# Turning rows with DMA transposes in SBUF instead of TensorE, and one output product moved, in a hybrid attention/gMLP encoder block

## The reference

```
a = rmsnorm(x) @ w_in                  -> q (512), k (128), v (128), zu (512), zv (512)
attn = windowed attention, 8 query heads on 2 kv heads, +-128 tokens, ALiBi, sink logits
sgu  = gelu(zu) * (w_s @ layernorm(gelu(zv)) + b_s)        (within chunks of 128 tokens)
h = x + concat(rmsnorm(attn), rmsnorm(sgu)) @ w_out
gate, val = rmsnorm(h) @ w_up          (2816 columns each; gate: convolution over 3 tokens)
h = h + (gelu(conv(gate)) * val) @ w_down
h = h + (p @ w_ple_proj) * sigmoid(rmsnorm(h) @ w_ple_gate)
out = rmsnorm(h) * g_final
```

## Time and profile before

| | us |
|---|---|
| median of 3 runs (slowest core) | 1627.82 (1625.87 to 1628.7) |
| the profiled execution, its own time | 1642.0 |
| its span on the slowest core (core 7) | 1640.4 |
| its span on the fastest core (core 3) | 1617.9 |
| TensorE matmul busy, core 7 | 1556.9 (95%) |
| VectorE, ScalarE, GpSimd busy, core 7 | 929.4, 755.8, 433.3 |

### The profile page before, as it was taken

The page is one execution under the profiler, slowest core; times in us unless marked ns, Lnnn a source line. Parts: engine busy times, 40 slices in busy tenths (PEclk is TensorE's granted clock), DMA queues, the critical chain, the costliest instruction groups (busy, mean ns, idle before and its releaser), DMA issues.

```text
span 1640.4 us, 32602 instructions; the slowest of 8 cores (1617.9 to 1640.4 us)
## 1 busy us (share of the span) xinstructions
PE 1556.9 (95%) x11608; PEld 1038.4 (63%) x11608; DVE 929.4 (57%) x1765; ACT 755.8 (46%) x1351; POOL 433.3 (26%) x816
## 2 busy tenths in 40 slices
PE   1899998999998999999999999999999999999997
PEld 1455555555554775867768577685766857668573
DVE  1555556566565654745647466474654746556464
ACT  2554555565565443534435344353543535434242
POOL 2345556565553310111101111011111101110011
PEclk9887899999999999999999999999999999999998
DMA  9745446453328931120211102021120211201011
GB/s 175 157 103 119 105 128 128 130 122 89 89 65 166 202 89 39 43 65 17 82 34 48 56 26 81 19 64 46 37 81 15 67 39 43 81 9 48 14 43 52
DMA packets 32495, 123.78 MB, mean 75 GB/s; under 512 B 4144, under 2 KB 6352, under 8 KB 30288
## 3 DMA queue, kind: packets, MB, share of 16 engines
q1 hardware_dynamic: 24096, 85.22, 15.7%
q0 software_dynamic: 8240, 36.49, 14.3%
HBM read 124.62 MB, written 33.55 MB: 96 GB/s over the span
## 4 chain that ended last, share of the span: by engine, by line
PE 86%; DMA 6%; ACT 3%; issue 2%; DVE 2%; POOL 0%; DVEq 0%; POOLq 0%; ACTq 0%; SPq 0%
PE ps L244 86%; DMA big<-w_in_b 2%; ACT big L244 2%; DVE big L244 2%; DMA hmid<-big 2%; DMA big<-w_down 1%; ACT L244 1%; POOL big L244 0%; POOL big L144 0%; DVEq L169 0%; POOLq L161 0%; ACTq L169 0%; POOLq L169 0%; ACTq L161 0%; SPq L169 0%
## 5 line engine op out<-in xcount | busy, mean ns | idle before, releaser
L244 PE MATMUL ps<-big 128*128 128x256 bf16 (+5 forms) x11608 | 1556.9, 296 | 71.4 <-POOL big L244 31.8
L244 PEld LDWEIGHTS ps<-big 128*128 128x128 bf16 x11608 | 1038.4, 99 | 589.3 <-issue 157.4
L244 POOL TENSOR_SCALAR big<-big 128x1 f32<-128x1 f32 (+6 forms) x512 | 270.8, 534 | 1123.5 <-ACT big L244 1028.0
L244 ACT ACTIVATE big<-ps,big 128x256 f32<-128x256 f32 (+2 forms) x476 | 335.2, 707 | 330.9 <-PE ps L244 322.6
L244 DVE SCALAR_TENSOR_TENSOR big<-ps,big 128x256 f32<-128x256 f32 x704 | 338.7, 483 | 147.0 <-ACT big L244 108.0
L244 ACT ACTIVATE big<-big 128x256 bf16<-128x256 f32 (+3 forms) x553 | 317.8, 585 | 187.7 <-DVE big L244 174.6
L244 DVE TENSOR_TENSOR big<-ps,big 128x8 f32<-128x8 f32 (+3 forms) x176 | 146.9, 836 | 250.8 <-PE ps L244 243.6
L244 ACT ACTIVATE big<-ps 128x1024 bf16<-128x1024 bf16 (+2 forms) x96 | 78.0, 813 | 310.4 <-PE ps L244 308.5
L244 DVE SCALAR_TENSOR_TENSOR big<-big 128x1024 f32<-128x1024 f32 (+2 forms) x128 | 129.3, 1011 | 55.7 <-POOL big L244 46.9
L244 DVE TENSOR_TENSOR big<-big,ps 128x256 bf16<-128x256 bf16 x352 | 144.8, 411 | 5.6 <-ACT big L244 5.6
L244 POOL TENSOR_TENSOR big<-big 128x1 f32<-128x1 f32 (+1 forms) x224 | 126.5, 565 | 34.3 <-POOL big L244 1.7
(11 more groups left out here) (20 smaller groups left out, 32.3 us busy)
## 6 DMA issues: line engine op xcount, KB each, us to landing
big<-hmid SPq DMA_DIRECT2D x64, 512.0 KB, 6.2
big<-x SPq DMA_DIRECT2D x32, 512.0 KB, 3.7
hmid<-big SPq DMA_DIRECT2D x32, 512.0 KB, 2.9
out<-big SPq DMA_DIRECT2D x32, 512.0 KB, 3.1
big<-xT POOLq DMA_DIRECT2D x16, 512.0 KB, 6.7
big<-w_up POOLq DMA_DIRECT2D x8, 1024.0 KB, 12.8
big<-w_down POOLq DMA_DIRECT2D x2, 1792.0 KB, 22.5
big<-w_up POOLq DMA_DIRECT2D x4, 768.0 KB, 14.4
```

Of the source, the lines that this page charges most:

```text
L244: return S.op(eng, lambda e: getattr(e, fname)(*args, **kw), reads=r, writes=w, what=(fname, args, kw))
```

## The change

All three turnings are done by one DMA transpose each, from SBUF to SBUF, on SP's queue (`dmat`, which calls `dma_start_transpose`). So that one DMA can read a whole merged row, the attention half and the gMLP half now lie side by side in one buffer of 1024 (`mg_r`, two of them) in place of `aos_r` and `sgs_r`. `cT` gets 32 spare columns instead of 2, and its rows begin at column 16. `stat_ring` goes from 24 to 14 entries, and the four row-scale buffers `rsx_r`, each on a 64-byte place of its own before, become four slices of one buffer of 64 bytes (`rsx_t`). In stage 1 `OUT(b-2)` moves from before `SC(b,2)` to behind `PV(b)`.

```diff
+    def dmat(self, out, in_):
+        lane = self.lanes["sp"][self.lane_rr["sp"] % NLANE]
+        self.lane_rr["sp"] += 1
+        op = self._record(lane, "sp", lambda e: e.dma_start_transpose(out=out, in_=in_), [in_], [out], 16, what=("dma", (out, in_), {}))
+        op.signals = True
+        return op
...
-    stat_ring = Ring([alloc([16], F32) for _ in range(24)])
+    stat_ring = Ring([alloc([16], F32) for _ in range(14)])
...
-    aos_r = [alloc([512], BF16) for _ in range(2)]
-    sgs_r = [alloc([512], BF16)]
+    mg_r = [alloc([D], BF16)]
+    mg_r.append(alloc([D], BF16))
     mT_r = Ring([alloc([8, 128], BF16) for _ in range(2)])
-    rsx_r = [alloc([4], F32) for _ in range(4)]
+    rsx_t = alloc([16], F32)
+    rsx_r = [rsx_t[:, 4 * j:4 * j + 4] for j in range(4)]
...
     def T(n):
-        b = S.ps_pair()
-        aos, sgs = aos_of.pop(n), sgs_r[n % 2]
-        src = [aos[:, c * 128:(c + 1) * 128] for c in range(4)] + [sgs[:, c * 128:(c + 1) * 128] for c in range(4)]
-        pb = transp(src, None, b, 0)
         mT = mT_r.next()
         mT_of[n] = mT
-        I("dve", "tensor_copy", mT[:, :, :], pb.rearrange("p (c t) -> p c t", c=8), r=[ps(b)], w=[mT])
+        S.dmat(mT[:, :, :], mg_r[n % 2][:, :])
...
-    cT_r = [alloc([8, PW + 2], BF16) for _ in range(2)]
+    cT_r = [alloc([8, PW + 32], BF16) for _ in range(2)]
...
+    L = 16
     def prepT(b):
...
-        p = S.ps_pair()
-        pb = transp([cb[:, c * 128:(c + 1) * 128] for c in range(8)], None, p, 0)
         cT = cT_r[w % 2]
-        o = 1 + bb * 128
-        I("act", "activation", cT[:, :, o:o + 128], pb.rearrange("p (c t) -> p c t", c=8), AF.Copy, r=[ps(p)], w=[cT[:, :, o:o + 128]])
+        o = L + bb * 128
+        S.dmat(cT[:, :, o:o + 128], cb[:, :])
...
     def TD(b):
         db = db_of.pop(b)
-        p = S.ps_pair()
-        pb = transp([db[:, c * 128:(c + 1) * 128] for c in range(8)], None, p, 0)
         dT = dT_r.next() if b not in (NBLK - 3, NBLK - 1) else dT_x
         dT_of[b] = dT
-        I("dve", "tensor_copy", dT[:, :, :], pb.rearrange("p (c t) -> p c t", c=8), r=[ps(p)], w=[dT])
+        S.dmat(dT[:, :, :], db[:, :])
...
-                 (MIX, b - 1), (T, b - 2), (OUT, a - 2), (SC, b, 0), (PV, a), (SC, b, 1), (OUT, b - 2), (SC, b, 2),
-                 (UVZ, b), (PV, b), (UVZ, b + 1)]
+                 (MIX, b - 1), (T, b - 2), (OUT, a - 2), (SC, b, 0), (PV, a), (SC, b, 1), (SC, b, 2),
+                 (UVZ, b), (PV, b), (OUT, b - 2), (UVZ, b + 1)]
```

More of the change, by code:

```diff
@@ L313, in build_nc @@
     sinkb = alloc([8], F32)
-    sgs_r.append(alloc([512], BF16))
     assert top[0] <= C_OFF, top[0] - C_OFF
@@ L534, in PV @@
           r=[ps(b, 2), rden], w=[ao])
-        aos = aos_r[n % 2]
-        aos_of[n] = aos
+        aos = mg_r[n % 2][:, 0:512]
         rms_scale(ao, aos)
@@ L595, in MIX @@
         I("dve", "tensor_tensor", sgo[:, :], psb, gvu[:, 512:1024], ALU.mult, r=[psb, gvu], w=[sgo])
-        rms_scale(sgo, sgs_r[n % 2])
+        rms_scale(sgo, mg_r[n % 2][:, 512:1024])
     mT_of = {}
[L600 to L605, removed]
     def T(n):
-        b = S.ps_pair()
-        aos, sgs = aos_of.pop(n), sgs_r[n % 2]
-        src = [aos[:, c * 128:(c + 1) * 128] for c in range(4)] + [sgs[:, c * 128:(c + 1) * 128] for c in range(4)]
-        pb = transp(src, None, b, 0)
         mT = mT_r.next()
         mT_of[n] = mT
-        I("dve", "tensor_copy", mT[:, :, :], pb.rearrange("p (c t) -> p c t", c=8), r=[ps(b)], w=[mT])
+        S.dmat(mT[:, :, :], mg_r[n % 2][:, :])
     st_of = {}
@@ L644, in build_nc @@
     sg = alloc([D], F32)
-    cT_r = [alloc([8, PW + 2], BF16) for _ in range(2)]
-    top[0] = X_OFF + 8 * 4096 + 2 * 4096 + 128
+    cT_r = [alloc([8, PW + 32], BF16) for _ in range(2)]
     t1_r = Ring([alloc([PW], F32) for _ in range(2)])
     ge_r = Ring([alloc([PW], BF16) for _ in range(2)])
-    pT_r.append(alloc([2, PW], BF16))
+    assert top[0] <= R_OFF
     top[0] = R_OFF
@@ L653, in build_nc @@
     dT_r = Ring([alloc([8, 128], BF16) for _ in range(1)])
+    pT_r.append(alloc([2, PW], BF16))
     dT_x = S.sb_view(X_OFF, [8, 128], BF16)
@@ L693, in prepT @@
             if w % WPS == 0:
-                I("dve", "memset", cT[:, :, 0:1], 0.0, w=[cT[:, :, 0:1]])
+                I("dve", "memset", cT[:, :, L - 1:L], 0.0, w=[cT[:, :, L - 1:L]])
             else:
-                I("dve", "tensor_copy", cT[:, :, 0:1], oth[:, :, PW:PW + 1], r=[oth[:, :, PW:PW + 1]], w=[cT[:, :, 0:1]])
-                I("dve", "tensor_copy", oth[:, :, PW + 1:PW + 2], cT[:, :, 1:2], r=[cT[:, :, 1:2]], w=[oth[:, :, PW + 1:PW + 2]])
+                I("dve", "tensor_copy", cT[:, :, L - 1:L], oth[:, :, L + PW - 1:L + PW], r=[oth[:, :, L + PW - 1:L + PW]], w=[cT[:, :, L - 1:L]])
+                I("dve", "tensor_copy", oth[:, :, L + PW:L + PW + 1], cT[:, :, L:L + 1], r=[cT[:, :, L:L + 1]], w=[oth[:, :, L + PW:L + PW + 1]])
         elif w % WPS == WPS - 1:
-            I("dve", "memset", cT[:, :, PW + 1:PW + 2], 0.0, w=[cT[:, :, PW + 1:PW + 2]])
+            I("dve", "memset", cT[:, :, L + PW:L + PW + 1], 0.0, w=[cT[:, :, L + PW:L + PW + 1]])
     tail_u = [None]
@@ L710, in U @@
         for k in range(8):
-            I("pe", "matmul", pg[:, 0:PW + 2], wgt[:, k, o:o + 128], cT[:, k, :], start=(k == 0), stop=(k == 7),
-              r=[wgt[:, k, o:o + 128], cT[:, k, :]], w=[pg])
+            I("pe", "matmul", pg[:, 0:PW + 2], wgt[:, k, o:o + 128], cT[:, k, L - 1:L + PW + 1], start=(k == 0), stop=(k == 7),
+              r=[wgt[:, k, o:o + 128], cT[:, k, L - 1:L + PW + 1]], w=[pg])
         for k in range(8):
-            I("pe", "matmul", pv[:, 0:PW], wvl[:, k, o:o + 128], cT[:, k, 1:PW + 1], start=(k == 0), stop=(k == 7),
-              r=[wvl[:, k, o:o + 128], cT[:, k, 1:PW + 1]], w=[pv])
+            I("pe", "matmul", pv[:, 0:PW], wvl[:, k, o:o + 128], cT[:, k, L:L + PW], start=(k == 0), stop=(k == 7),
+              r=[wvl[:, k, o:o + 128], cT[:, k, L:L + PW]], w=[pv])
         t1 = t1_r.next()
```

## The result

The changed kernel takes 1694.26 us (median; 1692.3 at the lowest) where the kernel before takes 1627.79: a ratio of 1.0403 (95% interval 1.0373 to 1.0434), 66 us slower. The forecast was 1636 with a range up to 1680. Its direction was right, its size was not.

What follows compares the result with a forecast made beforehand. TensorE, busy 95% of the span, was taken as the bound. -42.7 + 17 + 27 + 2 + 2 + 3 = +8 on the profiled 1642.0 gave 1650, 14 lower for the runs' median: 1636 us, range 1606 to 1680.

Steps and rivals of the forecast that it cites:

- The work removed: Both stages: 96 turnings of eight TensorE transposes each go, -42.7 us at 0.445 us each.
- The cover of 10 us for `TD`: Stage 2: `TD(2w-1)` has 10.4 us between its issue and its use, so its transpose is hidden.
- X, 4.5 us: Cost of one DMA transpose of 256 KB from SBUF to SBUF, put at 4.5 us, between 2.9 and 26.5.
- The rival of long transposes: X of 10.5 us: `T(a-2)` late 3 to 4 us per iteration, `TD` late too; 1718 us; chance 20%.
- 8 us of cover, with the x^T and `w_up` loads beside it: hidden for X up to 8: Stage 1: `T(a-2)` goes at +1.3 us of the iteration, `OUT(a-2)` comes at +9.4; no wait expected.
- Between the stages, +27: Transposes queued on SP beside the `w_down` loads: `OUT(29)` waits 17 us, `U(0,0)` 5, `OUT(31)` 5.
- The new waits of stage 1, +17: Late exps of block b: +1.75 us per iteration, from waits before `UVZ(b)` and `PV(b)`, over iterations 1 to 14.
- The moved product's +1.25 - 0.8: Stage 1, `OUT(b-2)` moved: 1.25 us wait before `PV(b)`, 0.8 us given back at the iteration's head.
- The +3 for the lower clock: After gaps of this size TensorE returns at the lower clock for some us: +3 us.
- The +2 at the very end: End of stage 2: `TD(31)` has only 2.6 us in front of its use against 4.5: +2 us.
- The gap between the stages stays small: Rival: transposes slip between the weight packets, +5 us in place of +27, so 1614 us; chance 25%.
- No new waits: Rival: stage 1 exps cause no waits, 0 in place of +17 us, so 1619 us; chance 13%.

Runs made afterwards that it cites:

- run 5: Changed kernel with the old order (`OUT(b-2)` before `SC(b,2)`) and the seven turnings between the stages on TensorE: 1582.87 us, ratio 0.9688.
- run 1: Changed kernel with the old order, `OUT(b-2)` again before `SC(b,2)`: 1614.63 us, ratio 0.9907 to the kernel before.
- run 3: Changed kernel with each stage 1 `w_up` load issued behind `SC(b,0)` instead of at the iteration's end: 1638.29 us, ratio 1.0063.
- run 8: Changed kernel with the four row-scale buffers on 64-byte places of their own: 1689.51 us, ratio 1.0388.
- run 4: Changed kernel with the seven turnings between the stages (`prepT(0)` to `prepT(3)`, `T(29)` to `T(31)`) on TensorE: 1656.76 us, ratio 1.0162.
- run 6: Changed kernel, DMA transposes in stage 2 alone: 1610.14 us; kernel before with moved `OUT(b-2)` alone: 1629.73; that with shared row scales: 1633.55.
- run 7: Changed kernel with `w_up` and `w_down` laid out with a gap behind each row, so loads go in shorter pieces: 1703.61 us, ratio 1.0454.

## Why the prediction was right or wrong

- **The work removed** and stage 2: right, a little small. Forecast -42.7 us; by the stretches of run 5 against the kernel before, 17 us in stage 1 and 33 behind it, 50 in all. The cover of 10 us for `TD` held: TensorE waited for no transpose in stage 2.
- **X, 4.5 us**: right in kind. 3.0 with nothing else loading, 3.9 in the median of all. The estimate of 10.5 us from the page "VectorE: DVE Perf Modes" of the Trainium skill ("The three transpose paths") was not borne out: a whole row block of eight 128 x 128 pieces takes 3.0 us here. "X-Bar Transpose (TRN2)", in "Advanced Engine Details and Errata" of the Trainium skill, is nearer: 3.0 us for 256 KB stands beside 2.7 for the 512 KB store of `hmid`, as long as nothing else is loading. The rival of long transposes had the right symptom, `OUT(a-2)` late, for the wrong reason.
- **"8 us of cover, with the x^T and `w_up` loads beside it: hidden for X up to 8"**: this is the step that failed. The cover was right (8.5 us), the place was right (issued just behind the x load, as the new iteration begins), and the price was put at 0. But what has to be set against the cover isn't X; it is the landing beside the loads, 10.9 us in the median. It measured 58 us of waits in ten iterations, and some 20 us of lower clock behind them (the sixteen matmuls behind each wait took 4.8 to 6.2 us, against 3.45).
- **Between the stages, +27**: right cause, too small, and partly another path. The gap gave back 37.5 us when its seven turnings went to TensorE. The forecast had `OUT(29)` waiting 17 us for `T(29)`; TensorE stood 26.8 us in front of `MIX` because VectorE, which takes its work in order, stood at the edge column of `prepT(0)`, and then only 2.2 before `OUT(29)`. The forecast had SP's queue getting one packet for one of the load's, but no number of packets for a transpose; it is 64 per engine. With that number the wait is until the load ends, for the first transpose already. The other two places were forecast at 5 us each: 2.4 before `U(0,0)`, 12.4 before `OUT(31)`.
- **The new waits of stage 1, +17**: right in size, not in its parts. Without a `w_up` load an iteration takes 28.6 us in the changed kernel and 27.2 in run 1; over iterations 2 to 14, run 3 takes 17 us more than run 1. It is the shared scales that cost it: apart, in run 8, they bring 28.6 down to 27.2, 1.3 us as forecast. The moved product's +1.25 - 0.8 came to nothing: run 8 has the new order, run 1 the old, and both take 27.2. On the kernel before, the two edits together cost only 2.5 us.
- **The rest**: `T(0)` was forecast at +2, and iteration 2 begins 3.5 us later. The +3 for the lower clock was far under the 20 us above. The +2 at the very end wasn't told apart.
- **Sum by the stretches**: -33 (stage 2) - 17 (stage 1) + 17 (new waits, run 3 against run 1) + 54 (late transposes, the changed kernel against run 3) + 37 (between the stages) + 3.5 (start) = 61.5; the cores' medians differ by 62.5, the slowest cores, which the metric takes, by 66. The forecast's own sum, with the failed step at 0, was +8, and run 3, which takes that step's load away and keeps the rest, is at 1638.29 us, near the 1636. That is in part luck, since a gap too small by 10 us and a saving too small by 8 nearly cancel.
- **The rivals.** "The gap between the stages stays small" fell by run 4. "No new waits" fell by runs 1 and 8 for the changed kernel; on the kernel before (run 6) it nearly holds.

## What to carry to other kernels

In these runs a DMA's landing time held for a queue state, not for the operation. Before moving TensorE work to DMA transposes, lay every bulk load's time beside each transpose's issue time, and take, for those that meet, the end of the load as their landing. A DMA of many small packets loses most, since turns went by packets; shorter pieces in the load didn't help, as it then had as many of them (run 7). An order edit that costs nothing on its own can decide everything once a queue issues what the edit moved: 80 us here. And take the mean of several iterations before you price an edit: here two in a row differed by 1.85 us.

## What the runs showed of the hardware

- A DMA transpose of 128 x 1024 bfloat16 from SBUF to SBUF: 3.0 us from issue to landing with nothing else loading, 1.23 us of SP's time to issue, some 1024 packets of 256 B.
- Two queues with work on the same DMA engines sent equally many of the profile's packets, whatever their sizes: 72 and 73 (8 KB and 256 B), 251 and 251 (14 KB and 256 B, the changed kernel from 552 to 572 us), 460 and 459 (1 KB and 256 B).
- A transpose beside two loads of 1.8 MB, with one load of `hmid` rows ahead of it in its queue, landed after 27.5 us, nine times its own 3.0, and 0.8 us after the later of the two loads.
- Behind waits of 4.3 to 7.9 us, sixteen TensorE matmuls of 512 columns took 4.8 to 6.2 us, against 3.45 at full clock.
